# Eight modulation blocks of the second layer: chunks summed by VectorE, two sums contracted by TensorE

## The chip, the cores and the metric

One core of one Trainium2 chip runs the kernel. The metric is device time in microseconds (us) of one launch; before the change it is 1570.12 us, the median of 3 runs (1569.78 to 1570.47). Engines: PE is TensorE (PEld its weight loads), DVE is VectorE, ACT is ScalarE, POOL is GpSimd, SP is SyncE, which issues the loads.

## The reference, cut to what matters

A two-layer backbone over 640 tokens of width 1024 (512 latent, 128 context), all in fp32. Each layer is

```
m = silu(cond) @ ada_w[layer] + ada_b[layer]        # 6 x 1024 modulation values, cond is c or c_ctx
sh1, sc1, g1, sh2, sc2, g2 = split(m)
x = x + g1 * mixer(rmsnorm(x) * (1 + sc1) + sh1)     # layer 0: convolution and retention, layer 1: attention
x = x + g2 * (relu(h @ mlp_w1) ** 2 @ mlp_w2)        # h = rmsnorm(x) * (1 + sc2) + sh2
```

The modulation weights `ada_w` are 1024 x 6144 for each layer, and they meet only two vectors, `c` and `c_ctx`. With 1024 = 8 chunks of 128 rows, a modulation value is the sum over chunks k and partitions p of `silu(cond)[k, p] * ada_w[k, p, column]`.

## The kernel before, in words

Activations lie transposed (features on partitions, tokens along the free dimension) in `xT`; a product runs over 320 tokens (`HALF`) at a time into one PSUM bank, with each fp32 factor split into a high and a low fp32r part and three matmuls for each pair (`product`, L664). A weight tile lands in `raw` (even tiles) or `raw_high` (odd tiles), 512 KB for each of its halves j0 and j1; ACT makes the high part `wH`, POOL or DVE the low part `wL` (L1831 on POOL), and only then may SP load the next tile into the same place. SP works through one list of loads in order (`load_tile`, L503; `load_ada`, L515): a load that waits holds back all behind it.

**Modulation.** The first 16 of 96 output chunks are made at the start. The other 80 are made in 20 blocks of four chunks, each in two parts of 512 weight rows. `load_ada(p)` fetches part p (1 MB) into the one buffer `ada` when part p-1 has been used. `strips(p)` (L783) contracts it on PE: 4 chunks of 128 rows times 4 column tiles of 32, 16 matmuls of 128 columns with `siluc` (32 columns wide, two of them in use) as the stationary factor, all into bank 4. After part 1 of a block `modulation(block)` on DVE transposes the bank (L1984) and adds the bias. Blocks 0 to 7 come in layer 0's mixer, blocks 8 to 19 (parts 16 to 39) in layer 0's MLP, three parts in each of its eight cycles.

**The MLP.** Cycle c (0 to 7) makes 512 of the 4096 hidden features and multiplies them into `xT`. Cycles 0 and 1 are plain: eight PE groups of 24 matmuls for `w1`. In cycles 2 to 7 `w1` is a Strassen-Winograd product (`winograd`, L1083): seven products of 4 chunks, two groups of 12 matmuls each, in the order B11, T2, B21, T3, T1, T4, B22, with sums made by DVE in between (`combine`, `result`, L2357). I call a group of 12 matmuls a unit. Each cycle ends with 16 units for `w2` (L664, in four weight halves). DVE adds unit n into `xT` in `update(n)` (L1867). The units take turns in four banks, so unit n waits until update n-4 is done. In cycles 1 to 6 DVE also works between the updates on the next cycle's weights: four sums `t_sums` (L2345) after updates 6 to 9 and a low part `t_lo` (L2351) after update 11; in cycle 1 the operand splits `s_low` (L2323) after updates 1, 3, 4 and 5 as well.

Part numbers of the three places in a cycle: in `winograd` after B11 and after T3, and after unit 7 of `w2`. In SP's list of a cycle stand, in order, `w2` tile 0 (j0, j1), `w2` tile 1 j0, `w2` tile 1 j1, and `w1` of the next cycle (two tiles, j0 and j1 each); the three `load_ada` stand before the first, between the third and the fourth, and behind the fourth.

**Attention's output product.** After layer 1's attention PE runs 16 groups of 24 matmuls (`T_WO`), DVE `wo(n)` adds group n into `xT` and sums squares (`add_squares`, L1890 and L1892) for the next norm; `stat` (L794) on PE needs the squares of the first token half in the middle of the last groups.

Of the kernel before, what the change touches and what calls it, by code (L numbers as in the profile page):

```python
# [26 lines left out]
P = 128  # L27
# [8 lines left out]
EPS = 1e-6  # L36
CONV, WIDTH = 512, 31
# [137 lines left out]
MOD_LAYER0, MOD_ALL = (MOD1 - N_PRE) // 4, (2 * MOD1 - N_PRE) // 4  # L175
SHIFT_AT = (SH1, SH2, MOD1 + SH1, MOD1 + SH2)
# [3 lines left out]
R_C, R_NORM, R_CB, R_LG, R_LB = 0, 16, 48, 52, 56  # L180
# [32 lines left out]
def by_feature_chunk(inputs):  # L213

    out = np.zeros((P, 3, P), np.float32)
    for b, at, names in ((0, R_C, ("c", "c_ctx", "norm_g", "conv_dw_b", "conv_ln_g", "conv_ln_b")),
                         (1, 0, ("ada_b",)), (2, 0, ("conv_dw_w",))):
        for name in names:
            a = np.asarray(inputs[name]).reshape(-1, P)
            out[:, b, at:at + len(a)] = a.T  # L220
            at += len(a)
    return out


def hybrid_step(nc, x_prompt, x_sample, state_ret, cache_k, cache_v, ada_w, even_w_in, even_w_out, final_g,
# [3 lines left out]
    with ctx:  # L229
# [16 lines left out]
        ada = place("ada", [P, KC // 2, 512])  # L246
        const = place("const", [P, C_END])
# [6 lines left out]
        adaT = place("adaT", [P, 2, P])  # L254
# [104 lines left out]
        raw_high = nc.alloc_sbuf_tensor_at("raw_high", [P, 2, 1024], F32, offset=arena + 73248)  # L359
# [27 lines left out]
        sel = const[:, C_SEL:C_SEL + 2]  # L387
# [27 lines left out]
        ada_strips, ada_turn, mod_done = sem("ada_strips"), sem("ada_turn"), sem("mod_done")  # L415
        coef_done, pre_coef = sem("coef_done"), sem("pre_coef")
# [66 lines left out]

        block = ctx.enter_context(nc.Block())
# [3 lines left out]
        def _(sp):  # L488
# [20 lines left out]
            def load_ada(p):  # L509

                if p:
                    sp.wait_ge(ada_strips, p)
# [3 lines left out]
                             .rearrange("(k p) n -> p k n", p=P)).then_inc(ada_in, 16)  # L516

# [55 lines left out]
            def load_mlp(layer, first_tile):  # L573
# [15 lines left out]

                w1(0)  # L590
# [64 lines left out]
        def _(pe):  # L655
# [118 lines left out]
            def strips(p):  # L774

                block, part = p // 2, p % 2
                pe.wait_ge(ada_in, 16 * (p + 1))
# [8 lines left out]
                last.then_inc(ada_strips, 1)  # L786

# [286 lines left out]
            def winograd(layer, c, v, part):  # L1074

                s = WINO * layer + c - PLAIN
# [14 lines left out]
                part(0)  # L1091
# [6 lines left out]
                for m in range(2):  # L1098
                    if s % WINO:
                        pe.wait_ge(c_done, 8 * s - 1 + m)  # L1100
                    one(B21, A12, 6, m)
                wait_low(pe, "p", s, T3)
# [3 lines left out]
                part(1)  # L1106
                wait_low(pe, "p", s, T1)
                for m in range(2):
                    pe.wait_ge(u2_done, 2 * s + 1 + m)
                    one(T1, S1, 2, m)  # L1110
                wait_low(pe, "p", s, T4)
# [8 lines left out]
            def mlp(layer, norm):  # L1120
# [3 lines left out]
                def part(c):  # L1124
                    return lambda n: strips(M_MLP + 3 * c + n) if layer == 0 else None

                for c in range(CYCLES):
                    t, v, f, s = t0 + 4 * c, v0 + 16 * c, f0 + 8 * c, WINO * layer + c - PLAIN
                    hooks = {}
                    if c == 0:  # L1130
                        if layer == 0:
                            hooks = {5: [lambda: strips(M_MLP)], 7: [lambda: strips(M_MLP + 1)]}
                        tile_pair(t, hH, hL, lambda n: pe.wait_ge(dve_free, v0 - 3 + n) if n < 4 else pe.wait_ge(act_free, a0 + n - 3),
                                  lambda half, tile, k: pe.wait_ge(h_ready, 16 * norm + 8 * half + k + 1), hooks,
                                  inside=(2, 0, lambda: stat(norm, 1, SUMS)), joint=((0, 1), (2, 3), (4, 5), (6, 7)))
                    elif c < PLAIN:
                        for b in range(2):
                            if layer == 0:
                                hooks = {1: [lambda c=c, b=b: strips(M_MLP + 3 * c + b)]}
                            tile_t(t + b, hH, hL, lambda n: pe.wait_ge(dve_free, v - 3 + n) if b == 0 else  # L1140
                                   pe.wait_ge(act_free, a0 + 8 * c + n + 1), None, hooks)
                    else:
                        winograd(layer, c, v, part(c))
# [11 lines left out]
                    if c == CYCLES - 1:  # L1155
                        if layer == 0:
                            hooks = {1: [lambda: part(c)(2)]}
# [7 lines left out]
                    for q in range(4):  # L1165
# [12 lines left out]
                        if q == 1:  # L1178
                            part(c)(2)
# [1465 lines left out]
```

## Time and profile before

| | |
|---|---|
| median of 3 runs | 1570.12 us (1569.78 to 1570.47) |
| profiled execution, first to last instruction (span) | 1567.7 us |
| PE busy | 1546.3 us, 99% of the span |
| DVE busy | 986.4 us, 63% |
| ACT, POOL busy | 625.8 us (40%), 487.8 us (31%) |
| strips of parts 0 to 39, matmuls of L783 | 1280 instructions, 2.6% of the chain that ended last |
| granted TensorE clock, mean | 0.996 of full speed |

For the profiled execution the profile gives the span; the time of that launch itself is not listed beside it, and the runs' median lies 2.4 us above the span. The profile counts two matmul instructions for each fp32 matmul of L783 (32 in a strip of 16) and, with its weight loads, "x32" in the chain of waits stands for a strip. A busy PE is not PE at its peak: matmuls overlap, and a matmul of 320 columns shows 310 ns but the next one starts 147 ns later.

### The profile page before, as it was taken

Reading aid. Unit: us, or ns where it says so; the run is one execution under the profiler, and the core shown is the slowest. Engines: PE = TensorE matmul, PEld = TensorE weight load, DVE = VectorE, ACT = ScalarE, POOL = GpSimd, SP = SyncE. Lnnn points to the kernel's source line nnn. Section 1 sums busy time; section 2 is a strip of 40 time slices with the busy share of each in tenths; the row PEclk is TensorE's granted clock in tenths of the full one; section 3 lists DMA queues with packets and bytes.
Section 4 is the critical chain, followed back from the end, with each engine's and each line's share of the span. In section 5 each row is a group of like instructions: output and inputs, shape, how many; then the busy total and the mean of one; then the engine's idle time right before and its main releaser. Section 6 shows DMA issues by size and latency. Waiting matters only on the chain.

```text
span 1567.7 us, 28790 instructions
## 1 busy us (share of the span) xinstructions
PE 1546.3 (99%) x11992; PEld 1512.9 (97%) x11992; DVE 986.4 (63%) x1831; ACT 625.8 (40%) x1152; POOL 487.8 (31%) x350
## 2 busy tenths in 40 slices
PE   8999999999999999999999999999999999999998
PEld 7999999999999999999999999999999999999998
DVE  5348677675774755565555888773675755556555
ACT  5323333344432344234235534662433334523443
POOL 0233313314222344143235253101333334324431
PEclk9999999999999999999999999999999999999999
DMA  9454333313243344344343121001222132223212
GB/s 327 158 188 142 122 116 114 102 55 110 80 159 111 122 131 138 109 135 148 101 155 134 35 81 61 28 2 54 81 81 59 63 108 68 84 66 108 68 54 82
DMA packets 133410, 162.23 MB, mean 103 GB/s; under 512 B 4640, under 2 KB 108064, under 8 KB 133280
## 3 DMA queue, kind: packets, MB, share of 16 engines
q1 hardware_dynamic: 132048, 159.34, 31.6%
q8 instruction: 95, 1.56, 0.4%
q10 hardware_dynamic: 1232, 1.05, 0.2%
q14 instruction: 35, 0.29, 0.1%
HBM read 156.44 MB, written 3.93 MB: 102 GB/s over the span
## 4 chain that ended last, share of the span: by engine, by line
PE 90%; DVE 5%; ACT 2%; issue 1%; DMA 1%; SPq 0%; POOL 0%; DVEq 0%; ACTq 0%
PE ps L664 59%; PE ps L1083 19%; PE ps L783 3%; PE ps L1275 2%; PE ps L1223 1%; DVE ps L1906 1%; PE ps L920 1%; PE ps L953 1%; DVE hL L1917 1%; DMA pre_w<-in_ada_w 1%; PE ps L869 1%; DVE ps L1896 1%; PE ps L949 1%; DVE amx L2503 1%; ACT wH L1319 1%
## 5 line engine op out<-in xcount | busy, mean ns | idle before, releaser
L1831 POOL TENSOR_TENSOR wL<-raw,wH 128x512 fp32r<-128x512 f32 x212 | 314.7, 1509 | 708.5 <-ACT wH L1319 513.7
L664 PE MATMUL ps<-fH,wH 128*128 128x320 f32 x1024 | 318.8, 311 | 0.2 <-DVE fL L2289 0.2
L664 PE MATMUL ps<-fH,wL 128*128 128x320 f32 x1024 | 316.6, 309 | 0.0
L664 PE MATMUL ps<-fL,wH 128*128 128x320 f32 x1024 | 316.6, 309 | 0.0
L1867 DVE SCALAR_TENSOR_TENSOR xT<-ps,modT,xT 128x192 f32<-128x192 f32 (+1 forms) x456 | 183.3, 434 | 192.0 <-PE ps L664 190.1
L1831 POOL TENSOR_TENSOR wL<-raw_high,wH 128x512 fp32r<-128x512 f32 x124 | 164.2, 1349 | 338.5 <-ACT wH L1342 209.7
L664 PE MATMUL ps<-hH,wH 128*128 128x320 f32 x704 | 221.3, 314 | 1.9 <-DVE hL L1917 1.1
L664 PE MATMUL ps<-hH,wL 128*128 128x320 f32 x704 | 217.8, 309 | 0.0
L664 PE MATMUL ps<-hL,wH 128*128 128x320 f32 x704 | 217.7, 309 | 0.0
L664 PEld LDWEIGHTS ps<-fH,wH 128*128 128x128 f32 x1024 | 192.5, 188 | 3.4 <-DVE xT L1867 1.2
L664 PEld LDWEIGHTS ps<-fL,wH 128*128 128x128 f32 x1024 | 192.5, 188 | 0.1
L664 PEld LDWEIGHTS ps<-fH,wL 128*128 128x128 f32 x1024 | 192.5, 188 | 0.0
L664 PE MATMUL ps<-wH,hH 128*128 128x256 f32 x560 | 162.3, 290 | 2.5 <-POOL wL L1831 1.1
L664 PE MATMUL ps<-wL,hH 128*128 128x256 f32 x560 | 158.5, 283 | 0.0
L664 PE MATMUL ps<-wH,hL 128*128 128x256 f32 x560 | 158.5, 283 | 0.0
L1342 ACT ACTIVATE wH<-t_raw 128x1024 fp32r<-128x1024 f32 x48 | 50.8, 1059 | 226.6 <-PE ps L664 172.9
L664 PEld LDWEIGHTS ps<-hH,wH 128*128 128x128 f32 x704 | 132.3, 188 | 6.4 <-DVE hL L1917 2.8
L664 PEld LDWEIGHTS ps<-hL,wH 128*128 128x128 f32 x704 | 132.3, 188 | 0.2
L664 PEld LDWEIGHTS ps<-hH,wL 128*128 128x128 f32 x704 | 132.2, 188 | 0.0
L2289 DVE TENSOR_TENSOR fL<-fs,fH 128x320 fp32r<-128x320 f32 x128 | 92.0, 748 | 58.8 <-ACT fH L1642 52.3
L1083 PE MATMUL ps<-s,wH 128*128 128x320 f32 x576 | 127.9, 310 | 0.0
L1083 PE MATMUL ps<-hH,wH 128*128 128x320 f32 x384 | 119.4, 311 | 0.0
(269 smaller groups left out, 3093.7 us busy)
## 6 DMA issues: line engine op xcount, KB each, us to landing
ada<-in_ada_w SPq DMA_DIRECT2D x40, 1024.0 KB, 5.4
raw<-in_mlp_w SPq DMA_DIRECT2D x64, 512.0 KB, 3.8
raw_high<-in_mlp_w SPq DMA_DIRECT2D x64, 512.0 KB, 3.8
raw<-in_even_w_in SPq DMA_DIRECT2D x28, 512.0 KB, 5.9
pre_w<-in_ada_w SPq DMA_DIRECT2D x16, 512.0 KB, 9.1
raw<-in_odd_w_qkv SPq DMA_DIRECT2D x10, 512.0 KB, 3.5
raw<-in_even_w_out SPq DMA_DIRECT2D x8, 512.0 KB, 3.6
raw<-in_odd_w_o SPq DMA_DIRECT2D x6, 512.0 KB, 3.5
```

The lines of the kernel that those rows point to most:

```text
L664: last = nc.tensor.matmul(ps[:, bank, 0:width], a_, b_, start=(k == 0 and p_ == 0), stop=(k == nk - 1 and p_ == 2))
L783: last = nc.tensor.matmul(ps[32 * j:32 * j + 32, B_ADA, 0:P], siluc[:, 4 * part + k, :], by_lane[:, j], start=(part == 0 and k == 0), stop ...
L869: last = nc.tensor.matmul(ps[:, GATE_BANKS[n], 0:HALF], a_, b_, start=(k == 0 and p_ == 0), stop=(k == KC - 1 and p_ == 2))
L920: return nc.tensor.matmul(ps[:, bank, at:at + RV], kd_nat[:, r, tile, :], v_nat[:, tile, :], start=True, stop=True)
L949: last = nc.tensor.matmul(out, prob[:, cs], v_nat[:, tile, :], start=True, stop=ctx_)
L953: last = nc.tensor.matmul(out, qdec[:, r, cs], S[:, r, n, :], start=False, stop=(r == 1))
L1083: last = nc.tensor.matmul(ps[:, bank + m, 0:HALF], a_, b_, start=(k == 0 and p_ == 0), stop=(k == 3 and p_ == 2))
L1275: last = nc.tensor.matmul(ps[:, 6, cs], va[:, vt, kv * P:(kv + 1) * P], pT[:, h % 2, n, cs], start=(n == 0), stop=(n == 4))
L1342: nc.scalar.activation(wH[:, BLOCK_AT["p", s, i] % 4, :], src, ACT.Copy).then_inc(wh_done, 1)
L1831: last = nc.gpsimd.tensor_tensor(wL[:, at % 4, cs], raw(t)[:, j, cs], wH[:, at % 4, cs].bitcast(F32), ALU.subtract)
L1867: last = nc.vector.scalar_tensor_tensor(out=x, in0=ps[:, n % 4, c0 - half * HALF:c0 - half * HALF + w_], scalar=modT[:, gate_at + k, which ...
L2289: nc.vector.tensor_tensor(fL[:, k, halfcols(half)], fs[:, n % 2, :], fH[:, k, halfcols(half)].bitcast(F32), ALU.subtract).then_inc(f_ready, 1)
```

## The change

Blocks 10 to 15 and 18, 19 (`SUMMED`) are no longer contracted chunk by chunk on PE. DVE sums their weights over the eight chunks, once for each of the two condition vectors, in two buffers `ada_sum0` and `ada_sum1` of 128 x 512: `sum_step(i, j)` multiplies one chunk by that chunk's column of `siluc` (a scalar for each partition) and adds it. The weights come in parts of 256 rows (512 KB, two chunks) that take turns in the two halves of `ada`; a part has four steps (two chunks, two vectors), a block has four parts, 32 parts in all with 128 steps. `strips_of_sums(b)` then sums over partitions on PE: per sum four matmuls with `one_row`, 8 in place of 32 for a block. The other blocks (`FULL`) stay as they were, some at other places. `raw_high` moves to the end of SBUF, and `adaT` becomes one buffer.

```
+SUMMED = [*range(MOD_LAYER0 + 2, MOD_LAYER0 + 8), MOD_ALL - 2, MOD_ALL - 1]
+FULL = [p for p in range(2 * MOD_ALL) if p // 2 not in SUMMED]
+PART_MLP, PART_WO, PART_END = 0, 24, 32
+def PART_AT(c, slot):
+    return 4 * (c - 1) + slot if 0 < c < CYCLES - 1 else None
...
-        raw_high = nc.alloc_sbuf_tensor_at("raw_high", [P, 2, 1024], F32, offset=arena + 73248)
+        raw_high = nc.alloc_sbuf_tensor_at("raw_high", [P, 2, 1024], F32, offset=SB_END - 8192)
...
+            def load_part(i):                                   # SP
+                if i is None:
+                    return
+                if i in (PART_MLP, PART_MLP + 1):
+                    sp.wait_ge(ada_strips, M_MLP + 4)
+                elif i in (PART_WO, PART_WO + 1):
+                    sp.wait_ge(ada_strips, len(FULL))
+                else:
+                    sp.wait_ge(sum1_done, 2 * (i - 1))
+                m, row0 = N_PRE + 4 * SUMMED[i // 4] - MOD1, 256 * (i % 4)
+                sp.dma_start(ada_part(i), ...).then_inc(part_in[i % 2], 16)
...
                 for c in range(CYCLES):                          # load_mlp, SP
-                    if layer == 0 and c:
-                        load_ada(M_MLP + 3 * c)
+                    if layer == 0 and c == CYCLES - 1:
+                        load_ada(M_MLP + 16)
                     w2(c, 0, (0, 1))
                     w2(c, 1, (0,))
-                    if layer == 0 and c:
-                        load_ada(M_MLP + 3 * c + 1)
+                    if c == 1:
+                        parts(c, 0, 1)
+                    elif c:
+                        parts(c, 2)
                     w2(c, 1, (1,))
                     if layer == 0 and c == 0:
                         load_ada(M_MLP + 1)
-                    if layer == 0:
-                        load_ada(M_MLP + 3 * c + 2)
+                        load_ada(M_MLP + 2)
                     if c < CYCLES - 1:
                         w1(c + 1)
+                    if layer == 0 and c == 0:
+                        load_ada(M_MLP + 3)
+                    if layer == 0 and c == CYCLES - 1:
+                        for p in range(M_MLP + 17, M_MLP + 20):
+                            load_ada(p)
+                    if c == 1:
+                        parts(c, 2)
+                    if c:
+                        parts(c, 3)
+                        parts(c + 1, 0, 1)
...
             sp.wait_ge(sc_full, N_ATT)
+            load_part(PART_WO)
+            load_part(PART_WO + 1)
             load_tile(T_WO + 3, k8(odd_w_o[0], 768))
+            for i in range(PART_WO + 2, PART_END):
+                load_part(i)
             load_mlp(1, T_MLP1)
...
+            def strips_of_sums(b):                               # PE
+                pe.wait_ge(sum0_done, 8 * b + 8)
+                pe.wait_ge(sum1_done, 8 * b + 8)
+                pe.wait_ge(ada_turn, SUMMED[b])
+                pe.wait_ge(vec_in, 16)
+                for c, total in enumerate((ada_sum0, ada_sum1)):
+                    by_lane = total[:].rearrange("p (b j r) -> p j b r", j=4, r=32)
+                    for j in range(4):
+                        last = nc.tensor.matmul(ps[32 * j:32 * j + 32, B_ADA, 0:P], one_row[:, c], by_lane[:, j],
+                                                start=(c == 0), stop=(c == 1), tile_position=(0, 32 * j))
+                last.then_inc(sum_strips, 1)
...
+            def sum_step(i, j):                                  # DVE
+                k, c = j // 2, j % 2
+                total, done = ((ada_sum0, sum0_done), (ada_sum1, sum1_done))[c]
+                by, part = siluc[:, 2 * (i % 4) + k, c:c + 1], ada_part(i)[:, k, :]
+                if j == 0:
+                    dve.wait_ge(part_in[i % 2], 16 * (i // 2 + 1))
+                if i % 4 == 0 and k == 0:
+                    if i:
+                        dve.wait_ge(sum_strips, i // 4)
+                    nc.vector.tensor_scalar(total[:], part, by, None, ALU.mult).then_inc(done, 1)
+                else:
+                    dve.wait_ge(done, 2 * i + k)
+                    nc.vector.scalar_tensor_tensor(out=total[:], in0=part, scalar=by, in1=total[:],
+                                                   op0=ALU.mult, op1=ALU.add).then_inc(done, 1)
```

Where things now stand. Cycle c of 1 to 6 sums parts 4(c-1) to 4(c-1)+3, its slots 0 to 3, which make one block; PE contracts it in the next cycle, behind the first unit of B11 (`strips_of_sums(c - 2)` in cycles 2 to 7). On DVE, in cycles 2 to 6: slot 0 all four steps at the cycle's start behind `t_lo(T3)` and `modulation`, slot 1 steps 0 and 1 before the two `combine` of T3, steps 2 and 3 behind updates 1 and 2, slot 2 behind updates 3, 4, 5 and 10, slot 3 behind updates 12 to 15. In cycle 1:

```
+                        after = {0: [lambda: steps_of(c, 2, 0)], 2: [lambda: steps_of(c, 2, 1)],
+                                 10: [lambda: steps_of(c, 2, 2, 3)]}
+                    for j in range(4):
+                        after[12 + j] = [lambda j=j: steps_of(c, 3, j)]
```

with slots 0 and 1 of cycle 1 two steps at a time behind hidden groups 4 to 7. PE's strips in layer 0's MLP: parts 16 to 18 in cycle 0 and 19 in cycle 1 as before; in cycle 7 part 32 behind B21, 33 behind T1, 34 and 35 behind units 0 and 4 of `w2`. Before, a cycle from 1 on had three (2 more in cycle 1, 3 in each later one). Block 18 is summed in parts 24 to 27 (eight steps before `wo(0)`, two behind each of `wo(2)` to `wo(5)`), and contracted behind group 6; block 19 in parts 28 to 31 (two steps behind `wo(6)` and `wo(7)`, four behind each of `wo(8)`, `wo(9)`, `wo(10)`), and contracted in cycle 0 of layer 1's MLP.

## Rows read from the trace of the kernel before

**Rows 1.** The page's head, its busy times, its chain by engine

```profile
span 1567.7 us, 28790 instructions
...
PE 1546.3 (99%) x11992; PEld 1512.9 (97%) x11992; DVE 986.4 (63%) x1831; ACT 625.8 (40%) x1152; POOL 487.8 (31%) x350
...
PE 90%; DVE 5%; ACT 2%; issue 1%; DMA 1%; SPq 0%; POOL 0%; DVEq 0%; ACTq 0%
```

**Rows 2.** Chain of waits over the whole span: start us, us, what

```profile
537.74 3.52 PE ps L1083 x24
...
594.15 3.53 PE ps L1083 x24
...
597.68 1.01 PE ps L783 x32
...
819.83 3.53 PE ps L1083 x24
...
1289.52 24.64 PE ps L1083 x168
...
1342.43 24.63 PE ps L1083 x168
```

**Rows 3.** DVE in order of time, cycle 3: start us, us, instruction, [idle before]

```profile
600.75 0.49 DVE L2357 TENSOR_TENSOR u<-ps,p 128x320 f32<-128x320 f32 x1 [4.25 <-PE ps L1083]
...
607.79 0.49 DVE L2357 TENSOR_TENSOR u<-ps,u 128x320 f32<-128x320 f32 x1 [1.27 <-PE ps L1083]
...
609.96 2.68 DVE L2289 TENSOR_TENSOR fL<-fs,fH 128x320 fp32r<-128x320 f32 x2
...
650.62 0.68 DVE L1867 SCALAR_TENSOR_TENSOR xT<-ps,modT,xT 128x192 f32<-128x192 f32 x2 [1.08 <-PE ps L664]
```

**Rows 4.** Durations of two DVE lines: ns min/median/max, first and last start

```profile
L2101 DVE SCALAR_TENSOR_TENSOR qdec<-qT,qtab x8: 679/686/1783, 130.7 to 290.4; 128x512 f32<-128x512 f32 x8
...
L2289 DVE TENSOR_TENSOR fL<-fs,fH x128: 475/492/1637, 438.4 to 1528.7; 128x320 fp32r<-128x320 f32 x128
```

**Rows 5.** DVE in order of time, cycle 1

```profile
511.25 1.63 DVE L2289 TENSOR_TENSOR fL<-fs,fH 128x320 fp32r<-128x320 f32 x1 [1.72 <-ACT fH L1613]
...
512.81 1.00 DVE L1867 SCALAR_TENSOR_TENSOR xT<-ps,modT,xT 128x320 f32<-128x320 f32 x2
...
532.50 0.55 DVE L1867 SCALAR_TENSOR_TENSOR xT<-ps,modT,xT 128x320 f32<-128x320 f32 x1
```

**Rows 6.** POOL in order of time, cycles 1, 3, 7 and output product

```profile
509.99 6.57 POOL L1831 TENSOR_TENSOR wL<-raw_high,wH 128x512 fp32r<-128x512 f32 x4 [8.94 <-ACT wH L1319]
...
609.50 2.79 POOL L1831 TENSOR_TENSOR wL<-raw_high,wH 128x512 fp32r<-128x512 f32 x2 [18.14 <-ACT wH L1342]
...
835.18 2.79 POOL L1831 TENSOR_TENSOR wL<-raw_high,wH 128x512 fp32r<-128x512 f32 x2 [18.14 <-ACT wH L1342]
...
1095.60 5.05 POOL L1831 TENSOR_TENSOR wL<-raw_high,wH 128x512 fp32r<-128x512 f32 x4 [9.04 <-ACT wH L1319]
```

**Rows 7.** SP's issues in order of time, cycles 1 and 7

```profile
512.56 4.39 SPq L503 DMA_DIRECT2D raw_high<-in_mlp_w  x2
...
838.45 0.47 SPq L515 DMA_DIRECT2D ada<-in_ada_w  x1
```

**Rows 8.** DMA issues in 512:517, 615:617, 838:839: KB, us to landing

```profile
raw_high<-in_mlp_w SPq DMA_DIRECT2D x2, 512.0 KB, 3.8
...
raw<-in_mlp_w SPq DMA_DIRECT2D x1, 512.0 KB, 5.0
...
ada<-in_ada_w SPq DMA_DIRECT2D x1, 1024.0 KB, 5.7
```

**Rows 9.** Windows: stretch, its us, busy PE, PEld, DVE, ACT, POOL, clock

```profile
512.80:531.34 18.54, 18.54 (x151) 18.01 (x150) 18.37 (x30) 5.79 (x6) 8.79 (x4) 1.00 0.40 120
```

**Rows 10.** DVE in order of time, output product, wo(8)

```profile
1096.91 0.55 DVE L1867 SCALAR_TENSOR_TENSOR xT<-ps,modT,xT 128x320 f32<-128x320 f32 x1 [1.27 <-PE ps L664]
```

**Rows 11.** Chain of waits, output product

```profile
1110.07 0.54 PE ps L794 x2
```

More of the change, by code:

```diff
@@ L221, in by_feature_chunk @@
             at += len(a)
+    for c in range(2):
+        out[:, 0, R_ROW + 32 * c + c] = 1
     return out
@@ L1072, in _, with winograd @@
             S1, S2, S3, S4 = (lambda k, i=i: [s_hi[i][:, k, :], s_lo[i][:, k, :]] for i in (1, 2, 3, 4))
[L1074 removed]
+            def winograd(layer, c, v):
+                mod = layer == 0
                 s = WINO * layer + c - PLAIN
@@ L1090, in winograd @@
                     one(B11, A11, 0, m)
-                part(0)
+                    if mod and m == 0:
+                        strips_of_sums(c - 2)
                 wait_low(pe, "p", s, T2)
@@ L1101, in winograd @@
                     one(B21, A12, 6, m)
+                if mod and c == CYCLES - 1:
+                    strips(M_MLP + 16)
                 wait_low(pe, "p", s, T3)
@@ L1110, in winograd @@
                     one(T1, S1, 2, m)
+                if mod and c == CYCLES - 1:
+                    strips(M_MLP + 17)
                 wait_low(pe, "p", s, T4)
@@ L1142, in mlp @@
                     else:
-                        winograd(layer, c, v, part(c))
+                        winograd(layer, c, v)
                     def free(n):
@@ L1177, in mlp @@
                                       lambda k: [x[:, k, half * HALF:(half + 1) * HALF] for x in (fH, fL)])], 4, waits, HALF)
-                        if q == 1:
-                            part(c)(2)
+                        if q == 1 and layer == c == 0:
+                            strips(M_MLP + 2)
             mlp(0, 1)
@@ L2279, in mlp_layer, with steps_of, modulate @@
                 t0, q0 = (T_MLP0, T_MLP1)[layer], 8 * PLAIN * layer
-                def modulate(c, place):
-                    if layer == 0 and (c % 2 == 0 and place == 1 or c % 2 and place != 1):
-                        modulation(MOD_LAYER0 + (3 * c + place) // 2)
+                def steps_of(c, slot, *js):
+                    if layer == 0 and 0 < c < CYCLES - 1:
+                        for j in js:
+                            sum_step(PART_AT(c, slot), j)
+                def modulate(block):
+                    if layer == 0:
+                        modulation(MOD_LAYER0 + block)
                 def hidden_lo(c, n):
@@ L2561, in wo @@
                 residual(G_WO, V_WO, n, half, k, MOD1 + G1)
+            for i in (PART_WO, PART_WO + 1):
+                for j in range(4):
+                    sum_step(i, j)
             for n in range(8):
                 wo(n)
+                if n in (2, 3, 4, 5):
+                    sum_step(PART_WO + 2 + (n - 2) // 2, n % 2 * 2)
+                    sum_step(PART_WO + 2 + (n - 2) // 2, n % 2 * 2 + 1)
+                if n == 6:
+                    modulation(MOD_ALL - 2)
+                if n >= 6:
+                    sum_step(PART_WO + 4, n % 2 * 2)
+                    sum_step(PART_WO + 4, n % 2 * 2 + 1)
                 if n % 2 == 1:
```

91 lines of the change are left out of this document (63 added, 28 removed).

## The prediction

> **What bounds the kernel now.** First the page's head and its chain by engine [rows 1]: PE is busy 99% of the span and holds 90% of the chain that ended last, so a matmul that goes is time that goes, unless PE then waits. DVE is busy 63%: it has room on average, and the question is where. The chain over the span [rows 2] gives the clockwork. A cycle of layer 0 takes 594.15 - 537.74 = 56.41 us, one of layer 1, which has no strips, 1342.43 - 1289.52 = 52.91. Its first 14 units take 24.64 us, so a unit is 1.76 us. DVE in order of time [rows 3] shows its gaps: about 1.1 us before an update, 1.27 before a combine, 4.25 near the cycle's start.
>
> I write +t for us after a cycle's first matmul, and count from the profiled execution's span, 1567.7 us; the runs' median lies 2.4 us above it, and differences carry over.
>
> **PE's part.** Three strips cost 56.41 - 52.91 = 3.50 us, 1.17 each, of which 1.01 are its matmuls and 0.16 the change of work around them [rows 2]. Sixteen parts go: 16 x 1.17 = 18.7 us. A contraction of sums has half a strip's matmuls: 0.51 + 0.16 = 0.67 us, eight of them 5.4 us. All of this lies on PE. Net -13.4 us, in detail -2.34 in cycle 1, -2.83 in each of cycles 2 to 6, +1.84 in cycle 7, +0.67 twice in layer 1. Were the 0.16 paid twice in a contraction, once for each sum, it would be 1.3 us less; this is in the range.
>
> **What a step costs DVE.** No step is in the trace. The nearest row is a scalar_tensor_tensor of the same size with both tensors in SBUF: 679 ns least, 686 median, 1783 most [rows 4]. I take the median. Two updates of 0.55 us take 1.00 together [rows 5], so of back-to-back instructions some 0.08 overlap, and a step takes 0.60 of DVE's time. POOL stretches such an instruction: two low parts that usually take 0.49 take 2.68 together [rows 3, 4], just while POOL works, and POOL's own two pay only 0.25 (2.79, against 2.54 at 1.27 each) [rows 6]. I take 1.3 for a step that meets POOL.
>
> The Trainium skill says why ("SBUF — State Buffer", section "SBUF: two separate sides"): VectorE with two SBUF inputs and GpSimd take a port pair in turn, each for a whole instruction. This speaks against the change, since all but 16 of the 128 steps are of that kind. By the rule a step waits at most for one instruction of POOL; if none ever waited, the sum below would be about 1 us lower. The trace agrees with its 2.68.
>
> **Cycles 2 to 6.** Slot 0: t_lo(T3) ends at +2.7, the contraction at about +2.5, the modulation at +3.2, four steps at +5.7; T2's first combine is due at +5.9 (three units and 0.67). Slot 1's steps fit the 1.27 gaps, and POOL starts only at +15.5 [rows 3, 6]. Behind the updates a step of 0.60 and an update of at most 0.59 fit into 1.76. The last step is the delicate one, since PE waits for it behind B11's first unit, at +1.76: the last update starts at +0.04 [rows 3], the step at +0.63 and ends at +1.31. Margin 0.45; an earlier step under POOL can eat it. I count 0.3 us for all five cycles, 0 to 1.3. The loads hold nobody there: SP now stands before the `w2` loads until the last step is done, about 10 us longer than before, but ACT wants those weights only near +15.
>
> **Cycle 1.** Here the load is late. Part 2 is issued behind the four `w1` loads of cycle 2, and the last of these waits until POOL has made the low part of the tile before it; before it went out 4.39 us after 512.56, at the end of that entry [rows 7]. But DVE wants part 2 right behind update 0, with the other 15 updates queued behind that wait, and PE waits for these.
> In numbers: cycle 1's first half is 1.17 us earlier (one strip less), so POOL starts at 509.99 - 1.17 = 508.8. Its four instructions took 6.57 us, the last beside a long DVE sum that now comes later; alone they take 5.05 [rows 6]. I take the end at 514.4 (513.9 to 515.6). Part 2 is issued 0.45 later and lands in 3.8 us when alone, 5.0 close behind another [rows 8]: 514.4 + 0.45 + 4.5 = 519.4. DVE ends update 0 at 513.3 - 1.17 + 0.1 = 512.3 [rows 5] and stands still for 7.1 us (5.4 to 8.8). PE's unit 5 is due at 537.74 - 2.34 - 11 x 1.76 = 516.0 and needs update 1, now at 520.5. The queue does not catch up: DVE was already busy 18.37 of 18.54 us there [rows 9] and now has four more steps (2.4 us) less a modulation (0.6).
> Where it ends: update 12 started at 532.50 [rows 5]; less 1.17, plus 1.8, it starts at 533.1 even without the wait; four updates with their steps (0.47 or 0.59 + 0.60 each) end the last step at 537.8, and PE comes for it at 537.74 - 2.34 + 1.76 = 537.2. So 0.6 us without the wait. With it 7.1 more, less about 1 us that DVE's sums save because POOL has finished: +6.7 us on the end, 4.5 to 9.
>
> **Cycle 7.** Part 33 is now loaded behind `w2`'s last half tile, which waits for the low part of B22. In the trace the load at this place goes out at 838.45, +18.6, and lands 5.7 later [rows 2, 7, 8]. The first strip before it shrinks from 1.17 to 0.67, so +18.1 and a landing at +23.8. PE reaches strips(33) behind ten units, a contraction and strips(32): 17.6 + 0.67 + 1.17 = +19.5. It waits 4.3 us (3.6 to 5.0). Part 32 is in time: it waits for the last sum (+1.3), lands by +7, and is needed at +11.3. Parts 34 and 35 follow with 5.7 us each and land 2 to 3 us ahead of need.
>
> **The output product.** Loads 24 and 25 come while attention ends, eight steps fit before wo(0) matters (group 4 is the first to need it, 14 us in). Late is only the tail: four steps behind each of wo(8), wo(9), wo(10). wo(8) is at 1096.9 [rows 10], POOL works from 1095.6 for 5.05 us [rows 6]; so of the first four steps three meet POOL (1.3 each), and that chain, with a pair of square sums of 1.0, ends wo(11) and its squares about 1.7 us later than now, where `stat` is due 0.67 later (1110.07 before [rows 11]). I take +1.1 us, 0 to 2.5. The `w1` loads of layer 1 go out later behind parts 26 to 31, but land 6 us before their use. Block 19's contraction and modulation in the last MLP cost no more than the 0.67 counted.
>
> **Sum.** -13.4 + 0.3 + 6.7 + 4.3 + 1.1 = -1.0 us: a span of 1566.7, a median of 1569.1 us. The gain in cycles 2 to 6 is given back at two late loads.
>
> **Rivals.**
> A: the late part in cycle 1 doesn't reach PE, because four banks absorb it. Only the 0.6 stays of 6.7: -13.4 + 0.3 + 0.6 + 4.3 + 1.1 = -7.1, 1563.0 us. For it: unit 5 has 2.8 us of slack. Against: the earliest landing is 513.9 + 0.4 + 3.4, 517.7, DVE has no idle time behind it. Chance 0.13.
> B: neither load is late for PE, for a reason that I don't see in the queue's order: -11.4, 1558.7 us. Chance 0.05.
> C, slower: DVE becomes the bound at the cycle's end. It decides from a step of 1.2 us: then update and step exceed a unit's 1.76, and the last step passes +1.76. At 1.5 us (1.42 spaced) four updates fall 0.75 behind, the last step ends at 0.63 + 0.75 + 1.5 = +2.9, and PE waits 1.1 in each of five cycles: 5.6 in place of 0.3, so +4.3, 1574.4 us; at 1.78 more. For it: the 1783 and 1637 ns [rows 4]. Against: the median, and that POOL is idle around the boundary. Chance 0.13.
> D: all mechanisms as forecast but at their upper ends (9, 5, 2.5, 1.3): +4.4, 1574.5 us. Chance 0.06.
> The forecast has 0.63, its own range 1566 to 1572.
>
> About 0.2%, 3.1 us, is what a measurement of this kernel can tell from no change. Faster by more: A, B and 0.15 of the forecast's 0.63, in all 0.27. Slower by more: C and D and next to nothing of the forecast, 0.20. Within: 0.53. The range reaches from A to D, 1562.5 to 1574, and leaves B and the tails out.
>
> **What would show it.** Cycles 2 to 6 of 53.6 us each, PE without waits: else C. In cycle 1 DVE idle about 7 us before its first sum step with the DMA of `ada` as releaser, and PE waiting for `xT` of L1867 in small pieces: if DVE waits and PE doesn't, A. In cycle 7 PE waiting some 4 us for the DMA of `ada` ahead of the strip behind T1. `stat` in the output product about 1 us late. Steps of 0.69 us, 1.3 or more only beside POOL. A time below 1563 would mean that I misread SP's order; one above 1574 that DVE holds up PE where I saw gaps.

## The result, and the profile after

The changed kernel takes 1577.45 us (median, 1575.33 to 1577.73) beside 1569.95 for the kernel before (1569.73 to 1570.47), a ratio of 1.0048 [1.0036, 1.0060]. In a later set it took 1575.69 (1574.26 to 1577.76), ratio 1.0041 [1.0028, 1.0053]; over all nine runs its median is 1576.4. So it is slower by 0.4 to 0.5%, beyond the 0.2% that counts as no change, where 1569.1 and no change were predicted; 1577.45 lies outside the range of 1562.5 to 1574.0. The profiled execution is the fastest of its four: 1575.33 us, span 1573.5, which is 5.8 above [rows 1].

The head of its page and the chain by engine answer to [rows 1]:

```profile
span 1573.5 us, 28228 instructions
...
PE 1537.2 (98%) x11608; PEld 1505.3 (96%) x11608; DVE 1085.1 (69%) x1959; ACT 625.7 (40%) x1152; POOL 494.6 (31%) x350
...
PE 86%; DVE 7%; ACT 3%; DMA 1%; issue 1%; POOL 1%; SPq 1%; DVEq 0%; ACTq 0%
```

PE has 384 matmuls less and 9.1 us less busy time, yet the span is longer: PE's share of the chain went from 90% to 86%, DVE's from 5% to 7%. PE's waits, longest first (line, what it waited for: us in all, times, longest), name the new ones. The last is put down to "issue", for the profile shows no releaser; it ends at 546.98, 0.1 behind DVE's last sum step of block 10.

```profile
PE ps L722 <- DVE xT L1942: 4.6, 1, 4.6
PE ps L841 <- DMA ada<-in_ada_w: 4.4, 1, 4.4
...
PE ps L865 <- DVE ssum L1967: 2.0, 1, 2.0
...
PE ps L855 <- issue: 1.4, 1, 1.4
```

The chain over the whole span (start us, us, what), with the lines that answer to [rows 2], places them. L841 is a strip, L855 a contraction, L1155 and L722 are the products.

```profile
439.64 1.01 PE ps L841 x32
...
547.62 23.07 PE ps L1155 x156
570.70 28.20 PE ps L722 x192
598.89 1.75 PE ps L1155 x12
...
813.51 1.76 PE ps L1155 x12
...
831.45 5.97 DMA ada<-in_ada_w
837.47 1.94 PE ps L841 x32
839.41 7.91 PE ps L1155 x48
...
867.59 2.17 DVE ps L1971
...
1066.88 24.64 PE ps L722 x168
...
1099.82 4.79 DVE ada_sum L2088 x4
...
1134.96 2.17 DVE ps L1971
```

From these rows and the same ones of every run comes the table on which all that follows rests: four stretches between fixed instructions, in us. "Cycles 1, 2" runs from the MLP's first strip, which lies in cycle 0 (439.64 here), to cycle 3's first matmul (598.89); "cycles 3 to 6" to cycle 7's first matmul (813.51); "cycle 7" to the reciprocal behind its first statistics (867.59); "output product" from its first matmul (1066.88) to the reciprocal behind it (1134.96). The second row is the kernel before with only the prediction's price for PE's work put in (1.17 off for each strip that goes, 0.67 on for each contraction; cycle 7 has one strip and one contraction more).

| | cycles 1, 2 | cycles 3 to 6 | cycle 7 | output product |
|---|---|---|---|---|
| before | 155.41 | 225.68 | 46.13 | 65.03 |
| PE's prices alone | 150.24 | 214.36 | 47.97 | 65.70 |
| changed kernel | 159.25 | 214.62 | 54.08 | 68.08 |
| the same again, e1_after | 159.34 | 214.64 | 55.14 | 69.74 |

PE's prices hold where nothing waits: cycles 3 to 6 are 11.06 shorter, 11.32 were priced. The losses are 9.0 in cycles 1 and 2 (6.7 forecast), 6.1 in cycle 7 (4.3) and 2.4 in the output product (1.1). The start-up before the first stretch took 0.9 longer (439.64 against 438.74), and that is no part of the change: the same point lay at 438.3 to 440.0 in the runs below, whose edits all take effect behind it. What lies behind the last stretch took 1.1 longer, 0.67 of it priced. In all 3.84 + 7.95 + 3.05 + 0.9 + 1.06 - 11.06 = 5.7 of the span's 5.8.

In cycle 1, DVE in order of time (start us, us, instruction, [idle before]) shows the late load, and after it a DVE without any gap:

```profile
520.77 0.75 DVE L2088 SCALAR_TENSOR_TENSOR ada_sum<-ada,siluc,ada_sum 128x512 f32<-128x512 f32 x1 [7.20 <-DMA ada<-in_ada_w]
...
537.47 2.44 DVE L2088 SCALAR_TENSOR_TENSOR ada_sum<-ada,siluc,ada_sum 128x512 f32<-128x512 f32 x2
...
540.41 1.73 DVE L2460 TENSOR_TENSOR wL<-t_raw,wH 128x1024 fp32r<-128x1024 f32 x1
542.06 0.54 DVE L1942 SCALAR_TENSOR_TENSOR xT<-ps,modT,xT 128x320 f32<-128x320 f32 x1
...
546.14 0.74 DVE L2088 SCALAR_TENSOR_TENSOR ada_sum<-ada,siluc,ada_sum 128x512 f32<-128x512 f32 x1
```

DVE waits 7.20 us (7.1 forecast). Update 12, at 532.50 before [rows 5], starts at 542.06. Two steps and a low part lie where POOL works (537.95 to 541.05). PE waits 4.6 us for `xT` in one piece and 1.4 more ahead of the contraction, which starts 107.34 us behind the first strip; by PE's prices it would be 98.4. So all of the 9.0 is DVE's lateness. TensorE's clock fell behind the 4.6 us too:

```profile
522.00:528.00 6.00, 5.96 (x26) 5.96 (x27) 6.00 (x9) 0.00 (x0) 0.00 (x0) 0.60 0.00 0
```

This is a window row: the stretch, its us, busy PE, PEld, DVE, ACT, POOL (each with its instructions), granted clock, DMA share, GB/s. The low clock cost nothing here, as DVE was busy without a gap and set the pace; it was 1.00 again from 528 on, and stayed there behind the 1.4 us. In cycle 7 the windows show what came behind PE's wait for part 33:

```profile
837.50:840.00 2.50, 2.50 (x34) 2.02 (x35) 0.00 (x0) 0.00 (x0) 1.96 (x2) 0.50 0.03 7
840.00:845.00 5.00, 5.00 (x33) 5.00 (x33) 1.37 (x4) 1.05 (x3) 0.00 (x0) 0.91 0.65 210
```

After 4.4 us without a matmul TensorE runs at half its clock, the lower of its two levels, 1.2 GHz: the strip at 837.47 takes 1.94 us, where every other in this chain takes 1.01, and the next four units (48 matmuls) 7.91, where they take 7.23. That is 1.6 us that the prediction did not have (2.5 in e1_after: 1.93 and 8.77). The Trainium skill has the rule ("TensorE: Matmul & The Clock Gate", section "Part 1: The HAM clock gate (the "warmup" mystery)"): an idle TensorE is gated down to 1.2 GHz, a busy one runs at 2.4. The trace agrees, with its 0.50; the prediction left the rule out.

In the output product PE waits 2.0 us for `ssum` (2.1 in e1_after). Behind this wait the two executions of the same kernel differ; the windows, first of this one, then of e1_after:

```profile
1110.00:1130.00 20.00, 17.97 (x122) 17.55 (x121) 16.02 (x32) 11.50 (x19) 7.11 (x6) 1.00 0.39 125
```

```profile
1110.00:1130.00 20.00, 17.88 (x110) 17.34 (x109) 15.66 (x32) 9.30 (x15) 5.04 (x4) 0.91 0.36 114
```

PE is busy as long in both but does 12 matmuls less in the second: from 1115.66 to 1119.66 its clock was 0.57. That is the 1.7 us between 68.08 and 69.74. Of the six traces with this wait (1.9 to 2.1 us) three keep 1.00 and take 67.99 to 68.08 (the first, e3_part33_early, e5_fill), and three fall to 0.57 to 0.61 over some 4 us and take 69.53 to 69.74 (e1_after, e2_part2_early, e9_b10). These 1.7 and the 1.1 of cycle 7 are what the two spans, 1573.5 and 1576.0, differ by, less 0.3 of start-up. Where two traces are compared below, a difference of this kind is not the edit's.

### The profile page after: what moved, and what is told of

It is laid out like the page before. It is cut to its first block, busy times and chain, and to the rows that moved or that the text cites. A ratio compares the mean times of both kernels' runs of the same rounds, so it can differ in the third digit from the quotient of the medians.

```text
span 1573.5 us, 28228 instructions
## 1 busy us (share of the span) xinstructions
PE 1537.2 (98%) x11608; PEld 1505.3 (96%) x11608; DVE 1085.1 (69%) x1959; ACT 625.7 (40%) x1152; POOL 494.6 (31%) x350
## 3 DMA queue, kind: packets, MB, share of 16 engines
q1 hardware_dynamic: 132304, 159.34, 31.7%
## 4 chain that ended last, share of the span: by engine, by line
PE 86%; DVE 7%; ACT 3%; DMA 1%; issue 1%; POOL 1%; SPq 1%; DVEq 0%; ACTq 0%
PE ps L722 57%; PE ps L1155 18%; PE ps L1349 2%; PE ps L841 2%; PE ps L1297 1%; DVE xT L1942 1%; DVE ps L1981 1%; PE ps L991 1%; PE ps L1024 1%; DVE ada_sum L2088 1%; POOL wL L1906 1%; DVE hL L1992 1%; DMA ada<-in_ada_w 1%; PE ps L940 1%; ACT wH L1394 1%
## 5 line engine op out<-in xcount | busy, mean ns | idle before, releaser
L1906 POOL TENSOR_TENSOR wL<-raw,wH 128x512 fp32r<-128x512 f32 x212 | 319.1, 1531 | 699.1 <-ACT wH L1394 507.2
L722 PE MATMUL ps<-fH,wH 128*128 128x320 f32 x1024 | 319.4, 312 | 5.3 <-DVE xT L1942 4.6
L722 PE MATMUL ps<-fL,wH 128*128 128x320 f32 x1024 | 317.2, 310 | 0.0
L722 PE MATMUL ps<-fH,wL 128*128 128x320 f32 x1024 | 317.1, 310 | 0.0
L722 PE MATMUL ps<-hH,wH 128*128 128x320 f32 x704 | 221.2, 314 | 2.0 <-DVE hL L1992 1.3
L722 PE MATMUL ps<-hH,wL 128*128 128x320 f32 x704 | 217.5, 309 | 0.0
L722 PE MATMUL ps<-hL,wH 128*128 128x320 f32 x704 | 217.5, 309 | 0.0
L722 PEld LDWEIGHTS ps<-fH,wH 128*128 128x128 f32 x1024 | 193.1, 189 | 8.1 <-DVE xT L1942 5.3
L722 PEld LDWEIGHTS ps<-fL,wH 128*128 128x128 f32 x1024 | 193.2, 189 | 0.1
L722 PEld LDWEIGHTS ps<-fH,wL 128*128 128x128 f32 x1024 | 193.2, 189 | 0.0
L722 PE MATMUL ps<-wH,hH 128*128 128x256 f32 x560 | 162.1, 289 | 2.4 <-POOL wL L1906 1.1
L722 PE MATMUL ps<-wL,hH 128*128 128x256 f32 x560 | 158.3, 283 | 0.0
L722 PE MATMUL ps<-wH,hL 128*128 128x256 f32 x560 | 158.3, 283 | 0.0
L722 PEld LDWEIGHTS ps<-hH,wH 128*128 128x128 f32 x704 | 132.2, 188 | 6.7 <-DVE hL L1992 2.8
L722 PEld LDWEIGHTS ps<-hL,wH 128*128 128x128 f32 x704 | 132.2, 188 | 0.2
L722 PEld LDWEIGHTS ps<-hH,wL 128*128 128x128 f32 x704 | 132.2, 188 | 0.0
L1155 PE MATMUL ps<-s,wH 128*128 128x320 f32 x576 | 127.4, 308 | 0.0
L1155 PE MATMUL ps<-hH,wH 128*128 128x320 f32 x384 | 119.7, 312 | 0.0
```

The costliest lines, as they stand in the source:

```text
L722: last = nc.tensor.matmul(ps[:, bank, 0:width], a_, b_, start=(k == 0 and p_ == 0), stop=(k == nk - 1 and p_ == 2))
L1155: last = nc.tensor.matmul(ps[:, bank + m, 0:HALF], a_, b_, start=(k == 0 and p_ == 0), stop=(k == 3 and p_ == 2))
L1906: last = nc.gpsimd.tensor_tensor(wL[:, at % 4, cs], raw(t)[:, j, cs], wH[:, at % 4, cs].bitcast(F32), ALU.subtract)
```

## The experiments

Each comparison is against the kernel before on the same chip, with 5 to 11 executions of the edited kernel; the median of the kernel before was 1569.64 (e1, e2, e3, e5) and 1569.25 (the others). Differences between runs of different sets carry these 0.4 us, and 1576.4, the median of all nine executions of the changed kernel, is from two sets.

**The changed kernel again, and each late load alone.** `e1_after` has no edit.

> The changed kernel again, for its usual trace: the profiled execution took 1575.3 us and the three others 1577.2 to 1577.7. My theory (late loads): 1577.4 us, and a trace in which DVE waits some 7 us for part 2 in cycle 1, PE 4.4 us for part 33 in cycle 7 and 2 us for the square sums in the output product; the 2 us by which executions differ lie where the granted clock is at 1.2 GHz. Rival (VectorE's extra 77 us of work spread over all cycles): the same time, but with small waits of PE in each of cycles 2 to 6.

1575.69 (1574.26 to 1577.76), ratio 1.0041 [1.0028, 1.0053], 1.7 below the 1577.4 of the theory; its stretches stand in the table above. The trace has the three waits of the theory (DVE 7.27 for part 2, PE 4.6 for part 33, PE 2.1 for the square sums), and cycles 3 to 6 are as short as in the first trace, so the rival's small waits are not there. The traced execution, 1577.76, is the slowest of its five.

`e2_part2_early` issues part 2 before the four `w1` loads of cycle 2:

```diff
+                    if c == 1:
+                        parts(c, 2)
                     if c < CYCLES - 1:
                         w1(c + 1)
...
-                    if c == 1:
-                        parts(c, 2)
                     if c:
                         parts(c, 3)
```

> SP issues part 2 in cycle 1 ahead of the four w1 loads of cycle 2; nothing else changes. Late-load theory: DVE's wait of 7.2 us goes, and with it 7 to 8 us of the 9.0 us that cycles 1 and 2 lose against PE's own work: 1570 us. Rival (DVE has too much work in cycle 1, the wait only hides it): DVE stays behind and the contraction of the first sums still waits 5 us or more: 1575 us or above.

1572.62 (1570.71 to 1574.66), ratio 1.0019 [1.0010, 1.0027]: between the theory's 1570 and the rival's 1575. Cycles 1 and 2 take 155.70 in place of 159.34, so the edit takes away only 3.6 of the 9.1. DVE's wait is gone, and DVE in order of time shows what stands in its place:

```profile
512.39 1.31 DVE L2088 SCALAR_TENSOR_TENSOR ada_sum<-ada,siluc,ada_sum 128x512 f32<-128x512 f32 x1
...
516.72 1.20 DVE L2088 SCALAR_TENSOR_TENSOR ada_sum<-ada,siluc,ada_sum 128x512 f32<-128x512 f32 x1
...
531.29 2.44 DVE L2088 SCALAR_TENSOR_TENSOR ada_sum<-ada,siluc,ada_sum 128x512 f32<-128x512 f32 x2
...
534.24 1.71 DVE L2460 TENSOR_TENSOR wL<-t_raw,wH 128x1024 fp32r<-128x1024 f32 x1
535.87 0.54 DVE L1942 SCALAR_TENSOR_TENSOR xT<-ps,modT,xT 128x320 f32<-128x320 f32 x1
```

No row of DVE from 507.65 to 542.16 has an idle time. Update 12 starts at 535.87, where the prediction had 533.1 without the wait. The four steps behind it end at 540.68, PE, due at about 537.2, starts its contraction at 540.78. The windows of this run show what comes behind that halt:

```profile
536.00:540.00 4.00, 2.40 (x15) 1.91 (x13) 4.00 (x10) 1.50 (x2) 0.00 (x0) 1.00 0.19 73
540.00:544.00 4.00, 3.22 (x26) 3.05 (x27) 3.96 (x9) 0.00 (x0) 0.00 (x0) 0.68 0.49 132
544.00:548.00 4.00, 4.00 (x27) 4.00 (x26) 1.58 (x3) 1.39 (x2) 0.00 (x0) 0.89 1.08 369
```

PE is idle 2.4 us in these windows, and the clock falls behind it to 0.68 and 0.89; cycle 2's following 156 matmuls take 24.63 us against 23.07. So the 5.5 that are left are 3.8 of lateness (the contraction starts 102.24 us behind the first strip, 98.4 priced) and 1.6 of clock. Against the changed kernel the contraction comes 5.1 us earlier, but there the 156 matmuls behind it took 23.07: 1.6 of the gain goes into the clock.

`e3_part33_early` issues part 33 before the first of `w2`'s last tiles in cycle 7:

```diff
+                    if layer == 0 and c == CYCLES - 1:
+                        load_ada(M_MLP + 17)
                     w2(c, 1, (1,))
...
-                        for p in range(M_MLP + 17, M_MLP + 20):
+                        for p in range(M_MLP + 18, M_MLP + 20):
```

> SP issues part 33 in cycle 7 ahead of the last half tile of w2, as the kernel before had it; nothing else changes. Late-load theory: PE's wait of 4.4 us goes. Of the clock there are two theories. If it fell because PE stood still (0.50 granted in the 2.5 us after the wait, the strip 1.94 us for 1.01), the 1.8 us behind the wait go as well: 6.2 us less, 1571.2 us. If the fall has another cause, 4.4 us less, 1573.0 us, and a slow strip stays.

1569.62 (1568.00 to 1570.71), ratio 1.0000 [0.9991, 1.0008]: 6.1 below e1_after, where the theory with the clock said 6.2 and the one without it 4.4. So the late load of cycle 7 costs more than the 4.3 forecast. Cycle 7 takes 48.07 us, 0.1 from PE's prices; both strips of block 16 take 1.01 in its chain:

```profile
814.70 8.99 PE ps L1157 x60
823.69 1.01 PE ps L843 x32
824.70 7.23 PE ps L1157 x48
831.93 1.01 PE ps L843 x32
832.95 7.23 PE ps L1157 x48
```

**Is it the clock behind the wait?** `e5_fill` leaves the load late and lets PE do 19 empty matmuls of 128x128, whose result nobody reads, ahead of the strip that waits:

```diff
                 if mod and c == CYCLES - 1:
+                    for _ in range(19):
+                        nc.tensor.matmul(ps[:, 5, 0:P], ones[:], ones[:], start=True, stop=True)
                     strips(M_MLP + 17)
```

> The changed kernel with 19 matmuls of ones by ones (128 columns, some 4.2 us at full clock, result in an unused bank) on PE ahead of strips(33), where PE stands still for 4.4 us; the load stays late. If idleness is what lowers the granted clock, the strip and the 48 matmuls behind it run at full clock and 1.8 us go: 1575.6 us. If not, the same time as the changed kernel, 1577.4 us, or a little more for matmuls that end after the load.

1575.50 (1573.69 to 1576.28), ratio 1.0036 [1.0023, 1.0050]. The chain at the same place:

```profile
832.33 6.90 DMA ada<-in_ada_w
839.27 1.08 PE ps L841 x32
840.35 7.23 PE ps L1155 x48
```

At full clock (1.00 from 837.5 to 845) the strip takes 1.08 and the units 7.23, against 1.93 and 8.77 in e1_after, though the load landed 6.90 us after its issue and there 6.20. PE's wait is 1.1 us in place of 4.6, as the empty matmuls fill the rest. Cycle 7 takes 53.47 against 55.14, and against 54.08 in the first trace. So this one trace shows the mechanism. The median does not: it lies at the theory's 1575.6, but e1_after, without the edit, is only 0.2 above it, so it is inconclusive.

**The output product.** `e4_wo` spreads the steps over groups 2 to 10 and contracts block 18 one group earlier:

```diff
-                       {2: [lambda: strips_of_sums(6)]} if t else None)
+                       {1: [lambda: strips_of_sums(6)]} if t else None)
...
+            WO_STEPS = {2: 4, 3: 2, 4: 2, 5: 1, 6: 4, 7: 2, 8: 2, 9: 3, 10: 4}
```

> The changed kernel with the output product's sum steps laid out anew: 4, 2, 2, 1, 4, 2, 2, 3 and 4 steps in groups 2 to 10 in place of four behind each of the groups' ends, and block 18 contracted one group earlier. The layer's output product lost 3.05 us against before where 1.8 was predicted, with a wait of 2.0 us for the sums. Theory (the steps stand too close, TensorE waits for the last of them): the wait of 2 us goes, about 1574.4 against 1576.4 for the changed kernel. Rival (the 2 us are those of VectorE's whole work here, wherever the steps stand): 1576.4 unchanged, the wait only moves to another reader.

1573.59 (1571.80 to 1574.37), ratio 1.0027 [1.0017, 1.0037]: 2.8 below the nine runs' median. The output product takes 65.98 us, 0.3 from PE's prices, in place of 68.08 and 69.74; the wait for `ssum` is gone, and with it the low clock. What the layout before it had done stands in the changed kernel's DVE in order of time:

```profile
1099.82 5.39 DVE L2088 SCALAR_TENSOR_TENSOR ada_sum<-ada,siluc,ada_sum 128x512 f32<-128x512 f32 x4
...
1105.61 2.72 DVE L2088 SCALAR_TENSOR_TENSOR ada_sum<-ada,siluc,ada_sum 128x512 f32<-128x512 f32 x4
```

The first four steps, beside POOL's four instructions from 1098.05 on, take 5.39 us, the next four 2.72, and both stand ahead of the updates that PE's statistics wait for. The edit leaves nine steps in place of twelve behind wo(8) to wo(10). The earlier contraction came with it and was not tried alone.

**What the other 5.5 us of cycle 1 are.** `e8_half` is e2_part2_early with DVE's added work halved, all loads and PE instructions kept; it leaves out the second vector's sum.

```diff
+                w = 8 if c else 512
...
-                for c, total in enumerate((ada_sum0, ada_sum1)):
+                for c, total in enumerate((ada_sum0, ada_sum0)):
```

> As the kernel with part 2 issued early (1572.6), but the sum for the second vector is made over 8 columns of 512 only, and TensorE contracts the first sum twice, so the second sum is left out of the result. All loads, waits and TensorE instructions stay. Theory (the 5.5 us left in cycles 1 and 2 is VectorE's work): about half of VectorE's added work goes, cycles 1 and 2 lose at most 1 us, about 1568; and if the output product's wait is VectorE's too, 1566. Rival (loads or the contraction itself): 1572.6 unchanged.

1564.82 (1563.73 to 1566.43), ratio 0.9973 [0.9963, 0.9982]: 7.8 below e2_part2_early. Cycles 1 and 2 take 151.23, 1.0 above PE's prices, so the 5.5 are DVE's work; the output product takes 65.80, so its loss is DVE's too. It is 1.2 more than the theory with the output product said (1566). In the two traces the output product gives 3.7 in place of the theory's 2, since e2_part2_early's was one with the low clock, and cycle 7 was 1.3 shorter (53.89 against 55.18), though nothing was changed there.

`e9_b10` takes block 10 alone back to full strips in the changed kernel; its loads and the counts behind it follow:

```diff
-SUMMED = [*range(MOD_LAYER0 + 2, MOD_LAYER0 + 8), MOD_ALL - 2, MOD_ALL - 1]
+SUMMED = [*range(MOD_LAYER0 + 3, MOD_LAYER0 + 8), MOD_ALL - 2, MOD_ALL - 1]
```

> The changed kernel with one block taken back: block 10 goes over TensorE in full strips in cycle 1, as before the change, and blocks 11 to 15, 18 and 19 stay summed. Theory (all that cycles 1 and 2 lose, 9.1 us, comes of block 10's loads and sums there, and the rest is untouched): 1576.4 - 9.1 + 1.7 (the strips' 2.34 less 0.67 for the contraction) = 1569.0. Rival (the first summed block costs this wherever it starts, so block 11 in cycle 2 inherits it): 1574 or more.

1569.11 (1567.28 to 1569.99), ratio 0.9996 [0.9987, 1.0005], as the theory had it (1569.0). The chain has no wait in cycle 1:

```profile
439.88 1.01 PE ps L843 x32
...
538.89 24.64 PE ps L1157 x168
...
591.73 1.75 PE ps L1157 x12
```

Cycles 1 and 2 take 591.73 - 439.88 = 151.85; PE's prices give 155.41 - 3 x 1.17 = 151.90. The whole 9.1 us hang on block 10's loads and sums, and block 11 inherits nothing: cycles 3 to 6 take 214.58.

**All edits together, and a better place for the contraction.** `e6_all` has the edits of e2, e3 and e4; `e7_all_b10` those of e3, e4 and e9.

> All three edits together: part 2 issued early (-3.6 so far), part 33 issued early (-6.1), the output product's steps spread (-2.0 expected). Theory that they are independent losses: 1576.4 - 11.7 = 1564.7, under the kernel before. Rival (a gain in one stage is taken back in the next, as DMA and VectorE come earlier relative to TensorE): 1568 or more.

> As the last, but block 10 is not summed: its four chunks go over TensorE in full strips as in the kernel before, so VectorE has no steps in cycle 1. Theory (cycle 1's remaining 5.5 us is VectorE's own load there, beside GpSimd, and what the clock loses behind it): the whole loss of 9.1 us of cycles 1 and 2 goes and 2.3 us of TensorE work come back: 1576.4 - 9.1 + 2.3 - 6.1 - 2.0 = 1561.5. Rival (the 5.5 us come from the queue of loads around cycle 1, not from VectorE): about 1567.

1562.45 (1560.54 to 1562.93), ratio 0.9951 [0.9937, 0.9964], and 1559.12 (1558.40 to 1560.06), ratio 0.9935 [0.9923, 0.9948]. Both are 2.3 us below their theories, which had priced cycle 7 at 6.1 and the output product at 2.0. Against e1_after these stretches give 7.1 and 3.8, against the first trace 6.0 and 2.1; how often the changed kernel pays the low clock decides between them. Nothing is taken back by a later stage: the stretches are 155.70, 214.60, 48.09, 65.98 for the first and 151.85, 214.67, 48.08, 65.99 for the second. What remains in e6_all is cycle 1, where DVE finishes late. `e10_later` is e6_all with nothing changed but the place of block 10's contraction on PE, two groups of 12 matmuls later; `e11_later2` puts it three later.

```diff
-                    if mod and m == 0:
+                    if mod and m == 0 and c > 2:
                         strips_of_sums(c - 2)
...
                     one(T2, S2, 2, m)
+                    if mod and m == 0 and c == 2:
+                        strips_of_sums(0)
```

> The kernel with all three edits (1562.45), with TensorE's contraction of block 10 put later in cycle 2: behind the first half of the product T2 in place of the first half of B11, two groups of 12 matmuls later, 3.5 us. The sums, their loads and VectorE's order stay. Theory (VectorE ends the last sum 3.5 us after TensorE is there, and TensorE's halt and the lower clock behind it are the 5.5 us that cycles 1 and 2 still lose): most of that goes, 0.5 of it staying for the waits on xT ahead of the halt, so about 1557.5. Rival (VectorE is late for TensorE's own operands too, so another wait takes the place of this one): 1561 to 1562.5.

> As the last, with the contraction one more group later, behind the whole product T2. VectorE waits for it ahead of its next block's first sums. Theory: as the last or up to 1 us better if 3.5 us was just too little, 1557; rival (VectorE, which waits for the contraction ahead of its work of cycle 2, is made late for T3 and the halt comes there): 1560 or more.

e10_later: 1558.77 (1558.36 to 1560.03), ratio 0.9933 [0.9921, 0.9946], 3.7 below e6_all and 1.3 above its theory; e11_later2: 1559.79 (1559.09 to 1561.03), ratio 0.9940 [0.9927, 0.9952]. PE in e10_later works on while DVE ends its sums:

```profile
536.57 5.52 PE ps L1157 x36
542.09 0.57 PE ps L857 x16
542.66 2.39 PE ps L1157 x15
```

```profile
536.00:540.00 4.00, 3.85 (x26) 3.61 (x26) 4.00 (x10) 1.50 (x2) 0.00 (x0) 1.00 0.19 73
540.00:544.00 4.00, 4.00 (x40) 3.61 (x39) 3.07 (x8) 1.39 (x2) 0.00 (x0) 1.00 0.52 137
```

Beside the windows of e2_part2_early all but 0.15 of the idle 2.4 us is gone, and the clock stays at 1.00. Cycles 1 and 2 take 151.82 in place of 155.70: 3.9 of the 5.5 were PE's halt and the clock behind it. The other 1.6 stay, 1.2 of them as three waits for `fL` and `xT` (0.5, 0.5, 0.2); the theory had left 0.5 for these. Against e7_all_b10, summing block 10 saves two strips and costs this 1.6, and the two kernels' intervals overlap. Neither leaves work out, and both are 10 us below the kernel before. For e11_later2 cycles 1 and 2 take 152.53, 0.7 more, and its median is 1.0 above e10_later, with overlapping intervals: the theory's gain is not there. The rival's 1560 is not reached either, but its trace has one more wait of 0.5 us, for `fL` of DVE in `w2` of cycle 2 (564.12), which is of the kind that the rival named.

## Why the prediction was wrong

**PE's part: right.** 1.17 a strip and 0.67 a contraction give cycles 3 to 6 within 0.3 us of 225, e9_b10 cycles 1 and 2 within 0.1, e3_part33_early cycle 7 within 0.1. With the two loads, the output product and the place of one contraction mended, e10_later lies at 1558.77. Rival B, the same sum without late loads, had 1558.7; that the two agree so closely is in part luck, as e10_later has two edits more than B and its kernel before read 0.9 lower.

**Cycles 2 to 6: right.** 0.3 predicted; 0.26 in cycles 3 to 6, and PE without waits there. Rival C named DVE as the bound at each cycle's end. It does not happen in these cycles (the step is 745 ns, far from its 1.2 us). But in cycle 1 DVE is the bound, beside POOL with steps of 1.2 to 1.3 us, and there the prediction had counted 0.6 for it.

**Cycle 1: the step that failed.** The late load was read rightly: issued behind the `w1` loads, DVE still for 7.20 us against 7.1, and PE waiting for `xT`, though in one piece of 4.6 us and not in small ones. What failed is "So 0.6 us without the wait". e2_part2_early takes the wait away, and 5.5 remain. The working had eight steps at 0.60 in a stretch in which DVE was busy 18.37 of 18.54 us [rows 9], and let none of them meet POOL. Four of them lie ahead of update 12: the first two took 1.31 and 1.20, the next two 2.44 together, and `t_lo` beside them 1.71, while POOL worked (508.60 to 514.87, 515.71 to 519.08, 531.36 to 534.86). Above the free durations of 0.74, 1.47 and 1.21 that is 0.6 + 0.5 + 1.0 + 0.5, some 2.5, and update 12 is 535.87 - 533.1 = 2.8 late. A free step was also 0.745 us, not 0.68: the row that was taken [rows 4] is another operation of the same form. PE then halts, and in e2_part2_early the halt brings the lower clock, 1.6 us more.

In the changed kernel the same mis-sized steps stand behind the wait: the last two ahead of update 12 and `t_lo` meet POOL (2.44 and 1.73), the others run free. That is the larger part of the 9.0 - 6.7 = 2.3 that were missing; the clock has no share in it. The load and the overload do not simply add. Without the wait four of DVE's instructions more meet POOL (two steps and two of the splits `s_low`, 1.31, 1.20, 2.12 and 2.00 against 0.75, 0.74, 1.48 and 1.48), so 7.2 us of waiting move the contraction by 5.1, and the clock takes 1.6 of that back.

**Cycle 7: the mechanism right, the size short.** 4.3 predicted, PE's wait measured 4.4; 6.1 lost, since TensorE came back at 1.2 GHz (1.6 us of it). The clock stood in no term of the sum, though a wait of PE can bring it: 1.6 here, 1.7 in the output product of e1_after, nothing in that of the first trace.

**The output product: mis-sized.** 1.1 predicted, 0 to 2.5 its range, 2.4 measured, and 4.0 in e1_after, with the clock. The prediction had three of the four steps beside POOL at 1.3; they took 5.39 for the four, which is 1.35 each, and the eight that follow them 0.68 each, 5.46 together, where 4.8 were counted. e4_wo shows that spreading them, with the contraction one group earlier, is enough.

**The sum.** Predicted -1.0: -13.4 + 0.3 + 6.7 + 4.3 + 1.1. Measured for the profiled execution: -13.4 + 0.3 + 9.0 + 6.1 + 2.4 + 0.4 (behind the last stretch) + 0.9 (start-up) = +5.7. Rival D (all at their upper ends, 1574.5, +4.4) came nearest. Its 9 and 2.5 were met; it fell short by 1.1 in cycle 7, by 0.9 in the start-up and by 0.4 behind the last stretch, and had 1.0 too much in cycles 2 to 6. The median, 1577.45, lies 2.1 above the profiled execution, which was the fastest; e1_after's trace, of a launch of 1577.76, has its larger losses where the clock is low. The 0.20 given to slower was too little for a forecast whose three losses all lay on PE's path.

What stays open: why the clock behind the halt in cycle 7 cost 1.6 in one run and 2.5 in the next (1.4 in e8_half, 2.7 in e4_wo), and why it fell behind the same 2 us in three of six output products. The rows show that the clock came back at different times (0.91 against 0.73 from 840 to 845), not why.

## What to carry to other kernels

A wait of TensorE can cost more than its length, where it sets the time: price the work behind it at the lower clock too, from the kernel's own rows, and look at more than one execution. Of the cures, making the data earlier was worth most where one line in a queue did it (6 us in cycle 7); where the sums themselves were late, moving the waiting instruction two groups on gave 3.9. Filling the wait with empty matmuls kept the clock up, but gained nothing clear in the median. When work is moved into "idle gaps", look for the stretch in which the receiving engine has none, and lay each added instruction against the other engine's busy times there, not against the average. A load put behind others in one queue is late by what those wait for, and one step up in the queue was worth 6 us here.

## What the runs showed of the hardware

- TensorE's clock fell to 1.2 GHz behind waits of 4.4 us (0.50 from 837.5 to 840), and from 540 to 544 it was 0.68 behind idle pieces of 2.4 us in all (e2_part2_early); with 19 empty matmuls ahead of the same wait it stayed at 1.00.
- Behind a wait of 1.9 to 2.1 us it fell to 0.57 to 0.61 over some 4 us in three of six traces and stayed at 1.00 in the other three; behind 1.4 us ahead of the contraction it stayed at 1.00.
- A low clock cost nothing where DVE set the pace (0.60 from 522 to 528).
- A step of 128x512 in fp32 took 745 ns (733 least), 0.68 us each back to back, and up to 1791 ns beside POOL. In the first trace 45 of the 112 steps of L2088 ran beside POOL, 1.18 us on average; the other 67 took 733 to 752 ns.
- The start-up differs by 1.7 us between runs that are the same up to there (first strip at 438.3 to 440.0), which is as much as some of the edits are worth.
